# A recurrent mixer's keys and queries as one 128-column stationary block in a two-layer model

## What is computed

```python
def step(state, inp):
    r_t, w_t, k_t, v_t, kk_t, a_t = inp
    sa = jnp.einsum('bhij,bhj->bhi', state, -kk_t)
    state = (state * w_t[:, :, None, :] + sa[..., None] * (kk_t * a_t)[:, :, None, :]
             + v_t[..., None] * k_t[:, :, None, :])
    return state, jnp.einsum('bhij,bhj->bhi', state, r_t)
...
mean = jnp.mean(y, axis=-1, keepdims=True)
var = jnp.mean(jnp.square(y - mean), axis=-1, keepdims=True)
y = ((y - mean) * lax.rsqrt(var + RWKV_GN_EPS)).reshape(B, S, W) * ln_w + ln_b
```

## Time and profile before

| | |
|---|---|
| median of 3 runs | 1806.1 us (1806.1 to 1806.24) |
| profiled execution | 1804.95 us, its span 1803.6 us |
| TensorE busy | 1776.8 us, 99% of the span |
| VectorE busy | 1148.2 us, 64% |
| ScalarE busy | 944.1 us, 52% |
| GpSimd busy | 106.6 us, 6% |
| granted TensorE clock | 1.00 |

### The profile page before, as it was taken

The page is one execution under the profiler, slowest core; times in us unless marked ns, Lnnn a source line. Parts: engine busy times, 40 slices in busy tenths (PEclk is TensorE's granted clock), DMA queues, the critical chain, the costliest instruction groups (busy, mean ns, idle before and its releaser), DMA issues.

```text
span 1803.6 us, 26510 instructions
## 1 busy us (share of the span) xinstructions
PE 1776.8 (99%) x10850; PEld 1486.8 (82%) x10850; DVE 1148.2 (64%) x1581; ACT 944.1 (52%) x1429; POOL 106.6 (6%) x78
## 2 busy tenths in 40 slices
PE   9999999999999999999999999999999999999999
PEld 6888788878888888887888878888888888888887
DVE  5554589576555565555786755555696557696556
ACT  6454675345544454446653455444646554656553
POOL 0100010141000000000002210000000000000000
DMA  8755542223555567554421437555454456555453
GB/s 289 276 187 187 164 152 83 72 94 129 187 187 187 175 198 241 195 173 166 141 84 60 128 113 227 189 188 173 165 181 152 163 188 193 175 175 164 156 190 133
DMA packets 84344, 301.14 MB, mean 167 GB/s; under 512 B 9728, under 2 KB 10880, under 8 KB 83712
## 3 DMA queue, kind: packets, MB, share of 16 engines
q1 hardware_dynamic: 80192, 289.44, 48.7%
q10 hardware_dynamic: 3712, 8.56, 1.4%
q0 software_dynamic: 320, 1.45, 0.3%
HBM read 298.36 MB, written 1.05 MB: 166 GB/s over the span
## 4 chain that ended last, share of the span: by engine, by line
PE 89%; DVE 5%; ACT 3%; issue 1%; DMA 1%; SPq 0%; DVEq 0%; ACTq 0%
PE ps L396 25%; PE ps L398 25%; PE ps L397 25%; DVE wlo L376 2%; PE ps L619 1%; PE ps L1261 1%; PE ps L868 1%; PE ps L417 1%; PE ps L419 1%; PE ps L418 1%; ACT whi L335 1%; PE ps L1249 1%; DMA raw<-stream 1%; PE ps L2653 1%; PE ps L456 1%
## 5 line engine op out<-in xcount | busy, mean ns | idle before, releaser
L376 DVE TENSOR_TENSOR wlo<-raw,whi 128x1024 fp32r<-128x1024 f32 (+1 forms) x545 | 663.6, 1225 | 374.4 <-ACT whi L335 372.9
L335 ACT ACTIVATE whi<-raw 128x1024 fp32r<-128x1024 f32 (+1 forms) x545 | 570.9, 1053 | 457.1 <-PE ps L398 425.8
L396 PE MATMUL ps<-whi,a_hi 128*128 128x512 f32 x1680 | 667.7, 397 | 7.0 <-DVE a_lo L1991 2.0
L398 PE MATMUL ps<-whi,a_lo 128*128 128x512 f32 x1680 | 655.4, 390 | 0.0
L397 PE MATMUL ps<-wlo,a_hi 128*128 128x512 f32 x1680 | 654.3, 389 | 0.0
L396 PEld LDWEIGHTS ps<-whi,a_hi 128*128 128x128 f32 x1680 | 315.6, 188 | 75.8 <-issue 3.6
L398 PEld LDWEIGHTS ps<-whi,a_lo 128*128 128x128 f32 x1680 | 315.4, 188 | 67.5
L397 PEld LDWEIGHTS ps<-wlo,a_hi 128*128 128x128 f32 x1680 | 315.9, 188 | 61.6
L396 PE MATMUL ps<-whi,h_hi 128*128 128x512 f32 x336 | 131.6, 392 | 0.0
L398 PE MATMUL ps<-whi,h_lo 128*128 128x512 f32 x336 | 130.8, 389 | 0.0
L397 PE MATMUL ps<-wlo,h_hi 128*128 128x512 f32 x336 | 130.8, 389 | 0.0
(11 more groups left out here) (326 smaller groups left out, 1642.1 us busy)
## 6 DMA issues: line engine op xcount, KB each, us to landing
raw<-stream SPq DMA_DIRECT2D x545, 512.0 KB, 3.4
arena<-rows ACTq DMA_DIRECT2D x2, 1026.0 KB, 14.8
arena<-mem_turned ACTq DMA_DIRECT2D x2, 1024.0 KB, 9.3
arena<-lora ACTq DMA_DIRECT2D x2, 768.0 KB, 6.3
arena<-x_turned SPq DMA_DIRECT2D x4, 256.0 KB, 6.0
x_res<-x SPq DMA_DIRECT2D x2, 512.0 KB, 9.1
arena<-mem ACTq DMA_DIRECT2D x1, 1024.0 KB, 12.8
arena<-rows ACTq DMA_DIRECT2D x2, 512.0 KB, 5.1
```

The costliest lines, as they stand in the source:

```text
L335: self.split_hi.mark(act.activation(self.weights(self.whi, u), self.weights(self.raw, u), ACT.Copy), u)
L376: self.split_lo.mark(dve.tensor_tensor(self.weights(self.wlo, u), self.weights(self.raw, u), self.weights(self.whi, u).bitcast(F32), ALU.s ...
L396: pe.matmul(out, a_h, hi, start=start, stop=False, skip_group_check=True)
L398: last = pe.matmul(out, a_l, hi, start=False, stop=True, skip_group_check=True)
```

## The change

The keys and queries of a chunk are laid out beside each other, so that one stationary block of 128 columns holds both, and one product with the state gives the right-hand side on the partitions 0 to 63 of a bank and the queries' part of y on 64 to 127. Chunk 0 uses bank 4, chunk 1 bank 7. The separate queries' product is taken out. The value products and y's products with U go to the partitions that this asks for; the eight for y of step (1,0) move from the T product of (1,1) to the state product of (0,1). The centring of y is made for each chunk by itself, on 64 partitions, four times a layer, with waits of TensorE for it before the state product of (0,1) and the T product of (1,0) in place of the one before the queries' product of (1,0).

```diff
@@ places1
-        self.AR, self.BK = self.mem(2, 4, S), self.mem(2, 4, S)
+        ar, self.BK = self.mem(8, S), self.mem(2, 4, S)
+        self.AR = ar.rearrange("p (h t) (q x) -> p h (t q) x", h=4, q=4).rearrange("p h (c a) x -> p h c a x", a=2)
@@ rw_within
-        co, hc = slice(c * HD, (c + 1) * HD), slice(h * HD, (h + 1) * HD)
-        return self.nc.tensor.matmul(self.bank(4 if which == 2 else 7)[co, hc], self.MK[co, t, h, which, :],
+        co, hc, o = slice(c * HD, (c + 1) * HD), slice(h * HD, (h + 1) * HD), HD * (which == 3)
+        return self.nc.tensor.matmul(self.bank((4, 7)[c])[o:o + HD, hc], self.MK[co, t, h, which, :],
@@ pe_rw_rhs
-            for i in range(4):
-                ins = pe.matmul(self.bank(4)[co, i * P:(i + 1) * P], self.AR[:, 0, i, cols], self.ST[:, i, :],
-                                start=False, stop=True, skip_group_check=True)
+        for i in range(4):
+            ins = pe.matmul(self.bank((4, 7)[c])[:, i * P:(i + 1) * P],
+                            self.AR[:, i, 2 * t + c, :, :].rearrange("p a x -> p (a x)"), self.ST[:, i, :],
+                            start=False, stop=True, skip_group_check=True)
@@ pe_rw_early
-        if t and c == 0:
-            pe.wait_ge(*self.rw_dve("gn centred", l, 0))
-        if t or c:
-            for i in range(4):
-                pe.matmul(self.bank(7)[co, i * P:(i + 1) * P], self.AR[:, 1, i, cols], self.ST[:, i, :],
-                          start=c == 0 and i == 0, stop=False, skip_group_check=True)
@@ pe_rw_u
+        if t == 1 and c == 0:
+            pe.wait_ge(*self.rw_dve("gn centred", l, 0, 1))
         for h in range(8):
             hc = slice(h * HD, (h + 1) * HD)
+            if c == 0:
+                self.rw_within(l, t, 1, h, 3, True)
+            elif t == 0:
+                self.rw_within(l, 0, 0, h, 3, False)
             ins = pe.matmul(self.bank(5)[co, hc], self.T2[t][co, 0, 4 * (h % 2) + h // 2, :], self.RHS[co, hc], start=True,
                             stop=True, skip_group_check=True)
-            self.rw_within(l, t, 1 - c, h, 3, c == 0)
@@ pe_rw_state
+        if t == 0 and c:
+            pe.wait_ge(*self.rw_dve("gn centred", l, 0, 0))
         if t == 0 or c == 0:
             for h in range(8):
                 hc, po, i = slice(h * HD, (h + 1) * HD), HD * (h % 2), h // 2
+                if t == 0 and c:
+                    self.rw_within(l, 1, 0, h, 3, True)
                 ins = pe.matmul(self.bank(6)[po:po + HD, i * HD:(i + 1) * HD], self.BWE[co, t, hc], self.U[co, hc],
@@
-            ins = pe.matmul(self.bank(7)[co, hc], self.MK[co, t, h, 1, :], self.U[co, hc],
+            ins = pe.matmul(self.bank((4, 7)[c])[HD:P, hc], self.MK[co, t, h, 1, :], self.U[co, hc],
@@ dve_rw_centre
-    def dve_rw_centre(self, l, t):
-        dve, m, MU = self.nc.vector, self.rw_dve, self.MU[t]
-        dve.wait_ge(*self.rw_pe("y", l, t, 1))
+    def dve_rw_centre(self, l, t, c):
+        dve, m, MU = self.nc.vector, self.rw_dve, self.MU[t][c][HD:P]
+        y = self.bank((4, 7)[c])[HD:P, :].rearrange("p (h d) -> p h d", h=8)
+        if t == 0 and c == 0:
+            dve.wait_ge(*self.rw_pe("u", l, 0, 1))
+        else:
+            dve.wait_ge(*self.rw_pe("y", l, t, c))
@@ pe_mix
         self.pe_rw_rhs(l, 1, 1)
-        self.pe_rw_early(l, 1, 1)
         self.pe_wo_a_turn(l, 0)
@@ dve_mix
+        self.dve_rw_centre(l, 0, 0)
         self.dve_rw_chunk(l, 0, 1)
-        self.dve_rw_centre(l, 0)
+        self.dve_rw_centre(l, 0, 1)
         self.dve_kv_norm(l, 1)
         self.dve_split(2)
         self.dve_rw_squares(l, 0)
         self.dve_rw_chunk(l, 1, 0)
+        self.dve_rw_centre(l, 1, 0)
         self.dve_split(1)
         self.dve_rw_norm(l, 0)
         self.dve_turn(("wo_a", l), 2, (2, 3))
         self.dve_turn(("wo_a", l), 2, (2, 3), kt0=2)
-        self.dve_rw_centre(l, 1)
+        self.dve_rw_centre(l, 1, 1)
```

More of the change, by code:

```diff
@@ L233, in places1 @@
         self.wc = sm[:, 224:240].rearrange("p (h c) -> p h c", h=4)
-        self.bonus, self.var, self.MU = ([sm[:, o + 8 * t:o + 8 * t + 8] for t in range(NT)] for o in (240, 256, 272))
+        self.bonus, self.var = ([sm[:, o + 8 * t:o + 8 * t + 8] for t in range(NT)] for o in (240, 256))
+        self.MU = [[sm[:, o + 8 * t:o + 8 * t + 8] for o in (272, 408)] for t in range(NT)]
         self.bonus2 = sm[:, 240:256]
@@ L1110, in dve_rw_keys @@
                 dve.wait_ge(*self.rw_act("length", l, i // 2))
-            m.mark(dve.scalar_tensor_tensor(A[:, i, :], K[:, i, :], self.pv(PV_KK, i), self.SQ[:, i, :], ALU.mult,
+            m.mark(dve.scalar_tensor_tensor(A[:, i], chunks(K[:, i, :]), self.pv(PV_KK, i), chunks(self.SQ[:, i, :]), ALU.mult,
                                             ALU.mult), "kk", l, i)
@@ L1114, in dve_rw_keys @@
         dve.wait_ge(*m.last())
-        m.mark(dve.tensor_tensor(B, A, self.AT, ALU.mult), "b w", l)
+        split = lambda x: x.rearrange("p h (c x) -> p (h c) x", c=4)
+        by_chunk = self.AR.rearrange("p h c a x -> p (h c) a x")[:, :, 0, :]
+        m.mark(dve.tensor_tensor(split(B), by_chunk, split(self.AT), ALU.mult), "b w", l)
         dve.wait_ge(*self.rw_act("exp cum", l, 1))
@@ L1132, in dve_rw_queries @@
         by_chunk = lambda x: x.rearrange("p h (c x) -> p (h c) x", c=4)
-        m.mark(dve.tensor_tensor(by_chunk(self.AR[:, 1]), by_chunk(self.RT), self.E1, ALU.mult), "r w", l)
+        queries = self.AR.rearrange("p h c a x -> p (h c) a x")[:, :, 1, :]
+        m.mark(dve.tensor_tensor(queries, by_chunk(self.RT), self.E1, ALU.mult), "r w", l)
     def act_rw_bonus(self, l):
@@ L1314, in pe_rw_early, with pe_rw_first @@
-    def pe_rw_early(self, l, t, c):
[L1316 to L1320, removed]
+    def pe_rw_first(self, l):
+        pe = self.nc.tensor
+        pe.wait_ge(*self.rw_dve("T", l, 1, 5))
+        pe.wait_ge(*self.rw_act("by token", "v", l, 1))
+        pe.wait_ge(*self.rw_act("by token", "k", l, 1))
+        for h in range(8):
+            for half in range(2):
+                ins = self.rw_within(l, 0, half, h, 2, True)
+        self.rw_pe.mark(ins, "rhs", l, 0, 0)
@@ new lines, in pe_rw_rhs @@
+    def pe_rw_rhs(self, l, t, c):
+        pe = self.nc.tensor
+        pe.wait_ge(*self.rw_before(l, t, c))
+        for i in range(4):
+            ins = pe.matmul(self.bank((4, 7)[c])[:, i * P:(i + 1) * P],
+                            self.AR[:, i, 2 * t + c, :, :].rearrange("p a x -> p (a x)"), self.ST[:, i, :],
+                            start=False, stop=True, skip_group_check=True)
+        self.rw_pe.mark(ins, "rhs", l, t, c)
+    def pe_rw_early(self, l, t, c):
+        pe, co = self.nc.tensor, slice(c * HD, (c + 1) * HD)
+        for h in range(8):
@@ L1364, in act_rw_chunk_rhs @@
         act.wait_ge(*self.rw_pe("rhs", l, t, c))
-        self.rw_act.mark(act.activation(self.RHS[co, :], self.bank(4)[co, :], ACT.Copy), "rhs", l, t, c)
+        self.rw_act.mark(act.activation(self.RHS[co, :], self.bank((4, 7)[c])[0:HD, :], ACT.Copy), "rhs", l, t, c)
     def act_rw_chunk_u(self, l, t, c):
```

32 lines of the change are left out of this document (10 added, 22 removed).

## The result

Eight executions of the changed kernel have a median of 1813.17 us (1811.83 to 1820.07), eight of the kernel before, the first three of them those of the table above, 1806.17 us (1804.97 to 1809.65): ratio 1.004, 95% interval 1.0027 to 1.0053. It is slower, by 7.0 us. The profiled execution took 1811.83 us, span 1810.3 us, against 1804.95 and 1803.6 before: 6.9 us more, 6.7 in the span. Lines have moved by some: L396 to L398 of before are L398 to L400 of after, VectorE's split L376 is L378, L1310 is L1317, L1322 is L1326, L1337 is L1341, L1295 is L1300, L1349 is L1356, L1358 (y's products) is L1365, ScalarE's copy L1365 is L1372, L1391 is L1398, L1447 to L1451 (the centring) are L1457 to L1461, L1469 and L1471 (the norm) are L1479 and L1481, a_lo's L515 is L517, L2103 is L2113.

What follows compares the result with a forecast made beforehand. TensorE carries 89% of the chain, but VectorE sets the restart: -1.10 + 1.77 + 0.34 = +1.0 us a layer, two layers +2.0 on the median 1806.1, giving 1808.1 us; range 1804.0 to 1811.5.

Steps and rivals of the forecast that it cites:

- same: Outcome from 1802.5 to 1809.7 us, within about 0.2% (3.6 us) of no change; chance 0.68.
- the slower case: Outcome above 1809.7 us; chance 0.24.
- Removed queries' product, widened block: Three steps a layer lose 1.02 us of TensorE each, 6.1 us in the kernel; the 128-column block costs nothing.
- Gain of 0.82 us at (0,1), ScalarE late: T product of (0,1) starts at 355.17 instead of 355.99, held by ScalarE's copy; 0.82 us gained of 1.02.
- Same-column pairs at no cost: First group and T product of (0,1): matmuls now sharing 64 columns cost nothing; rival of sequential pairs 1812.1, chance 0.07.
- Value products +0.51 us: Eight value products moved into the state product of (0,1), ahead of VectorE's mark, lengthen it by 0.51 us.
- State update of (1,0) 1.1 us earlier: VectorE's state update in step (1,0) starts 1.1 us earlier, as TensorE's state product and VectorE's queue both move up.
- Centring +1.77: The (1,0) half of y's centring, between state update and split on VectorE's chain, adds 1.77 us a layer.
- Split +0.34: VectorE's weight split lies entirely in the stretch slowed by GpSimd: 2.25 us against 1.91, +0.34.
- Behind the restart all shifts as one: Behind TensorE's restart at L2103 order and work stay the same, so everything only shifts; no added cost.
- a rival: TensorE's clock slows in the roughly 4 us idle stretch before the restart: 2.0 us a layer, 1812.1; chance 0.15.
- The median as the base: The run median 1806.1, 1.15 above the profiled execution, was the base for adding 2.0 us, giving 1808.1.

Runs made afterwards that it cites:

- the last experiment: Changed kernel with the (1,0) centring late, the second norm step behind VectorE's turns, and eight value products moved to y's products behind the state product; 1797.61 us.
- the filled kernel: Changed kernel plus three 128x512 products on constants, read by nothing, behind the T product of (1,1) in TensorE's idle stretch; 1806.8 us.
- the kernel before with a wait of 2.5 or 2.9 us: Kernel before plus two or four unread 128x512 reductions on VectorE behind the state update of (1,0); 1812.37 us with two, 1813.38 with four.
- the late centring: Changed kernel with the centring of (1,0) moved behind VectorE's turns, directly ahead of that of (1,1); 1806.13 us.
- the kernel with the values behind: Eight value products moved behind VectorE's mark, to y's products; 1804.45 us with only (1,0)'s centring late, 1797.61 with turns first too; which is not said.

## Why the prediction was wrong

The range ended at 1811.5, the median came at 1813.2, and I had put 0.68 on "same"; the slower case had 0.24.

- *Removed queries' product, widened block*: right. 0.98 us for the wide block against 1.02; the loads are hidden, as L805 had said. A load is listed with 192 ns now and 137 before, and the step of the passes did not grow. By the rule of the Trainium skill ("TensorE: Matmul & The Clock Gate", LDWEIGHTS), worked out as an estimate, the 64 added columns cost a load 53 ns. The trace agrees with the growth, 55 ns, but not with the whole load (53 and 107 by the rule), and it shows that none of it reaches the passes.
- *Gain of 0.82 us at (0,1), ScalarE late*: right; 0.72 measured, with a wait of 0.26 us.
- *Same-column pairs at no cost*: right; the pairs of the T product of (0,1) still step 0.058 us.
- *Value products +0.51 us*: right in kind. The state update of (0,1) starts at 360.56; forecast 360.51. The state product of (0,1) takes 0.92 us to y's first product where it took 0.53, so 0.39 for the 0.51; by the last experiment they cost some 0.35 a layer.
- *State update of (1,0) 1.1 us earlier*: 1.02. *Centring +1.77*: 2.4, since its small scaling took 1.02 us beside GpSimd where I had taken 0.4. *Split +0.34*: 1.64 us, 0.27 shorter than before. The sum of the three was +1.0 a layer, measured +1.08 in layer 0: that it fits is luck, since the centring is 0.6 too low and the split 0.6 too high. Layer 1 adds 0.98. For the whole, the filled kernel's 1.9 us stand against the forecast's 2.0.
- *Behind the restart all shifts as one*: this is the step that failed. The passes behind it ran at half the clock, which cost 2.39 us in layer 0 and 2.79 in layer 1; the forecast's sum had nothing for it. I had the mechanism as a rival, priced with 2.0 us a layer from the kernel's first passes (slow although their clock is listed as 1.00), which gave 1812.1, and gave it 0.15, since no row of the trace shows a fall later on. The forecast itself said that idle time would grow from 1.27 to 4 us; with a wait three times as long as any of its kind in the trace, the absence of falls in it was no evidence. Shown in its place: a mean clock of 0.990 to 0.996 in all eight executions of the changed kernel and 1.000 in all ten with the stretch filled, at nearly the same restart; and 0.997 or less in all nine of the kernel before with a wait of 2.5 or 2.9 us.
- *The median as the base*: I took the 1.15 us between the profiled execution and the median for an offset. The executions at 1.000 stand at 1803.8 to 1805.4, those at 0.999 from 1806.0; so the offset is falls of the clock too, and the narrow spread of three runs (1806.1 to 1806.24) hid it. With this base, the forecast's 2.0 us give 1806.9 without a fall, and the filled kernel has 1806.8.

## What to carry to other kernels

A step that lengthens TensorE's wait can cost twice: once the wait, and again the passes behind it at half the clock (1.08 and 2.39 us in layer 0 here). So look at how much TensorE does in the whole stretch around a wait, not at the wait alone, and where an edit thins it out, shorten the chain of the other engine in the same edit. Before an operation is put into another engine's queue, find the stretch in which that engine is the chain and place the operation behind it; here this centring and one norm step moved turned 7.0 us lost into 8.0 us won (1798.34 against 1806.35), and 8.7 with the value products moved.

## What the runs showed of the hardware

- The clock can fall with no single long wait: behind one of 1.01 us (the late centring), and at 336 to 341 us, where TensorE waits for no other engine, in some executions (stretch of the kernel with the values behind, clock 0.68):

```profile
336.00:340.00 4.00, 4.00 (x53) 0.68 0.00 0
```

  The Trainium skill ("TensorE: Matmul & The Clock Gate", Part 1: The HAM clock gate) says that the clock follows how busy TensorE was; the falls behind waits of 2.5 to 4.3 us agree. Those ahead of the recurrence come while TensorE is listed as busy all the time (4.00 of 4.00 us above); for them the runs show the place and no cause.
- A scaling of 64x8 on VectorE (L1459) takes 0.17 us when GpSimd is idle (at 378.79 us in the kernel with the late centring) and 0.49 or 1.02 beside it (at 362.07 and 372.46 us in the changed kernel), while the operation behind it, L1461, which reads PSUM, keeps its 0.69 us. So when an operation runs counts as well as how long it is: a weight split took 1.22, 1.64, 1.91 or 2.28 us.
